# VectorE turns k into token rows by 36 block transpositions; TensorE turns only v

## What is computed

```python
q, k, v, f, u, bg, cg, ga, gb = _split_cols(h @ w_in, IN_SIZES)   # k and v: 1024 columns, 16 heads x 64
o = lax.map(block, (qb, cb, pb))            # prompt attention over 256 tokens, with forget biases
k_past = cache_k[l][page_table].reshape(Bd, n_pages * PAGE_SIZE, N_HEADS, HEAD_DIM)
o = _sample_attention(q, k, v, cum_all[:, P:], cum_all, k_past, v_past)
kp_l.append(k); vp_l.append(v)              # prompt rows of k and v are outputs
ks_l.append(k); vs_l.append(v)              # and so are the sample rows
```

## Time and profile before

| | us |
|---|---|
| median of 3 runs | 1799.98 |
| lowest and highest | 1797.37 and 1800.78 |
| the profiled execution | 1800.58 |
| its span, first to last instruction | 1799.0 |
| TensorE busy | 1781.4 (99%) |
| VectorE busy | 904.7 (50%) |
| ScalarE busy | 702.3 (39%) |

### The profile page before, as it was taken

One profiled execution on the slowest core, in us unless ns is written; L12 is line 12 of the kernel. 1 busy time (PEld: TensorE's weight loads), 2 busy tenths in 40 slices (PEclk: granted clock), 3 DMA queues, 4 the chain that ended last, 5 costly groups with the idle time before them and its releaser, 6 DMA issues.

```text
span 1799.0 us, 31906 instructions
## 1 busy us (share of the span) xinstructions
PE 1781.4 (99%) x13658; PEld 1678.2 (93%) x13658; DVE 904.7 (50%) x1134; ACT 702.3 (39%) x823; POOL 26.1 (1%) x76
## 2 busy tenths in 40 slices
PE   8999999999999999999999999999999999999999
PEld 6888888897699999998979999999999999999999
DVE  4665662235644344454677344444444445565554
ACT  4433233335643333343354333333333334455454
POOL 0000100001000000000000000000000000000000
PEclk9999999999999999999999999999999999999999
DMA  9987677865654444458836554444444444444441
GB/s 361 393 356 319 225 306 308 346 236 208 242 190 166 164 164 164 164 198 339 327 139 259 193 204 164 164 163 163 163 163 163 163 163 165 165 164 165 165 164 74
DMA packets 59367, 382.38 MB, mean 213 GB/s; under 512 B 6989, under 2 KB 7861, under 8 KB 17159
## 3 DMA queue, kind: packets, MB, share of 16 engines
q1 hardware_dynamic: 57764, 378.27, 56.4%
q0 software_dynamic: 1328, 2.58, 0.4%
q10 hardware_dynamic: 178, 0.13, 0.0%
HBM read 376.15 MB, written 4.81 MB: 212 GB/s over the span
## 4 chain that ended last, share of the span: by engine, by line
PE 96%; DVE 2%; ACT 1%; issue 1%; DMA 1%; POOL 0%; DVEq 0%; ACTq 0%; POOLq 0%
PE bank L663 29%; PE bank L665 28%; PE bank L664 28%; PE bank L673 4%; PE bank L907 1%; DMA ada<-in_w_ada 1%; PE bank L1037 1%; PE bank L681 1%; PE bank L1006 0%; PE bank L692 0%; PE bank L1226 0%; PE bank L976 0%; ACT w_hi L1263 0%; PE bank L1149 0%; PE bank L886 0%
## 5 line engine op out<-in xcount | busy, mean ns | idle before, releaser
L663 PE MATMUL bank<-a_lo,w_hi 128*128 128x288 f32 x3632 | 1081.3, 298 | 4.0 <-DVE w_lo L1723 2.6
L664 PE MATMUL bank<-a_hi,w_hi 128*128 128x288 f32 x3632 | 1072.6, 295 | 0.0
L665 PE MATMUL bank<-a_hi,w_lo 128*128 128x288 f32 x3632 | 1069.0, 294 | 0.0
L1723 DVE TENSOR_TENSOR w_lo<-raw,w_hi 128x2048 fp32r<-128x2048 f32 x240 | 550.0, 2292 | 670.3 <-ACT w_hi L1263 669.7
L1263 ACT CAST w_hi<-raw 128x2048 fp32r<-128x2048 f32 x239 | 455.9, 1908 | 838.2 <-PE bank L665 816.9
L663 PEld LDWEIGHTS bank<-a_lo,w_hi 128*128 128x128 f32 x3632 | 681.6, 188 | 23.0 <-issue 22.0
L665 PEld LDWEIGHTS bank<-a_hi,w_lo 128*128 128x128 f32 x3632 | 684.8, 189 | 0.0
L664 PEld LDWEIGHTS bank<-a_hi,w_hi 128*128 128x128 f32 x3632 | 682.7, 188 | 0.0
L1833 DVE TENSOR_TENSOR a_lo<-hid,a_hi 128x1152 fp32r<-128x1152 f32 x44 | 59.4, 1352 | 12.3 <-ACT a_hi L1283 12.3
L673 PE MATMUL bank<-ada,cT 128*32 128x512 f32 (+1 forms) x608 | 63.3, 551 | 1.4 <-DMA ada<-in_w_ada 1.4
L1283 ACT CAST a_hi<-hid 128x1152 fp32r<-128x1152 f32 x44 | 50.7, 1155 | 0.0
(11 more groups left out here) (361 smaller groups left out, 973.1 us busy)
## 6 DMA issues: line engine op xcount, KB each, us to landing
raw<-in_w_ffn_in SPq DMA_DIRECT2D x88, 1024.0 KB, 4.8
raw<-in_w_in SPq DMA_DIRECT2D x75, 1024.0 KB, 8.4
ada<-in_w_ada SPq DMA_DIRECT2D x60, 1024.0 KB, 9.2
raw<-in_w_ffn_out SPq DMA_DIRECT2D x44, 1024.0 KB, 4.8
ada_o<-in_w_ada SPq DMA_DIRECT2D x24, 1024.0 KB, 9.0
raw<-in_w_o SPq DMA_DIRECT2D x16, 1024.0 KB, 5.0
ada<-in_w_ada SPq DMA_DIRECT2D x16, 512.0 KB, 11.0
raw<-in_cache_k SPq DMA_DIRECT2D x16, 512.0 KB, 4.3
```

The source lines that it names most:

```text
L663: pe.matmul(acc, w_hi[buf][:, a, cols], lo[:, kt, :], start=first and a == 0, stop=False)
L664: pe.matmul(acc, w_hi[buf][:, a, cols], hi[:, kt, :], start=False, stop=False)
L665: mm = pe.matmul(acc, w_lo[buf][:, a, cols], hi[:, kt, :], start=False, stop=last and a == tiles - 1)
L1723: tt(w_lo[buf][:, :, :], raw[s][:, :, :], w_hi[buf][:, :, :].bitcast(F32), ALU.subtract).then_inc(raw_turn, 1)
```

## The change

TensorE no longer turns k. The six tiles of k leave ROWS, and with them their 24 transpositions and the six copies out of PSUM (three on ScalarE, three on VectorE); what is left, now V_ROWS, is numbered anew. turn_suf waits for the sums alone. On VectorE turn_keys(b) turns a block of tokens from kT straight into k_rows, in SBUF: for each 32 tokens (t) and each 32 partitions (q) one instruction that transposes eight 32 x 32 blocks. It is called at u = 21, 22 and 23, behind that slot's split_lo where there is one: 16, 16 and 4 instructions. GpSimd's transfers of k_rows wait for k_turned. No product and no output changes.

```diff
@@ the lists @@
-    ROWS = ([("k", half, b) for half in range(2) for b in range(3)]
-            + [("v", 0, 0), ("v", 0, 1), ("v", 1, 0), ("v", 1, 1), ("v", 0, 2), ("v", 1, 2)])
-    ROW_BANK = (4, 5, 4, 5, 6, 7, 6, 7, 2, 3, 7, 2)
+    V_ROWS = [(0, 0), (0, 1), (1, 0), (1, 1), (0, 2), (1, 2)]
+    V_BANK = (6, 7, 2, 3, 7, 2)
+    QUAD = P // 4
@@ TensorE @@
             def turn_suf():
                 pe.wait_ge(suf_done, 1)
                 pe.wait_ge(cum_done, 1)
-                pe.wait_ge(rowT_a, 1)
-                pe.wait_ge(rowT_d, 1)
...
                 if mt == 1:
-                    pe.wait_ge(rowT_a, 3)
-                    pe.wait_ge(rowT_d, 3)
+                    pe.wait_ge(sufT_done, 1)
                     turn_k(0, (0, 1))
...
                     pe.wait_ge(ada_mods, ADA_MAIN + 1)
-                    pe.wait_ge(bank_turn, BT + MT * (G_QKV + 3))
-                    turn_rows(0)
-                    turn_rows(1)
                 if u == 20:
                     turn_suf()
-                if u == 21:
-                    pe.wait_ge(sufT_done, 1)
-                    pe.wait_ge(bank_turn, BT + MT * (G_QKV + 6))
-                    for n in range(2, 6):
-                        turn_rows(n)
@@ ScalarE @@
-                if u == 20:
-                    copy_row(act, nc.scalar.copy, 0)
...
-                if u == 22:
-                    copy_row(act, nc.scalar.copy, 2)
-                    copy_row(act, nc.scalar.copy, 4)
@@ VectorE @@
+            def turn_keys(b):
+
+                for t in range(min(P, NT - b * P) // QUAD):
+                    at_ = slice(b * P + QUAD * t, b * P + QUAD * t + QUAD)
+                    for q in range(4):
+                        rows = slice(QUAD * q, QUAD * q + QUAD)
+                        dst = k_rows[QUAD * t:QUAD * t + QUAD, b, :].rearrange("p (f n) -> p f n", n=P)[:, :, rows]
+                        ins = nc.vector.transpose(dst, kT[rows, :, at_])
+                ins.then_inc(k_turned, 1)
...
                     copy_sums()
-                    copy_row(dve, nc.vector.tensor_copy, 1)
-                if u == 22:
-                    copy_row(dve, nc.vector.tensor_copy, 3)
-                    copy_row(dve, nc.vector.tensor_copy, 5)
+                if u == 21:
+                    dve.wait_ge(bank_turn, BT + MT * (G_QKV + 6))
+                if u in (21, 22, 23):
+                    turn_keys(u - 21)
             copy_KT(0, 1)
             copy_KT(0, 3)
@@ GpSimd @@
-            pool.wait_ge(rowT_a, 3)
-            pool.wait_ge(rowT_d, 3)
+            pool.wait_ge(k_turned, 3)
             pool.dma_start(k_prompt[0, 0].rearrange("(b p) h d -> p b (h d)", p=P), k_rows[:, 0:2, :]).then_inc(s_kout, 16)
```

More of the change, by code:

```diff
@@ L374, in layer @@
         y_made = sem("y_made")
+        k_turned = sem("k_turned")
         rowT_ps, rowT_a, rowT_d, suf_ps, suf_done, sufT_ps, sufT_done = (sem(n) for n in (
@@ L418, in row_tile @@
         def row_tile(n):
[L420 to L424, removed]
+            half, b = V_ROWS[n]
+            return v_rows[half][:, b, :] if b < 2 else v_new[:, 512 * half:512 * half + 512]
         def copy_row(eng, copy, n):
@@ L429, in copy_row @@
             eng.wait_ge(rowT_ps, n + 1)
-            copy(dst, bank[ROW_BANK[n]][0:dst.shape[0], :]).then_inc((rowT_a, rowT_d)[n % 2], 1)
+            copy(dst, bank[V_BANK[n]][0:dst.shape[0], :]).then_inc((rowT_a, rowT_d)[n % 2], 1)
         def y_tile(n):
@@ L881, in turn_rows @@
             def turn_rows(n):
-                name, half, b = ROWS[n]
+                half, b = V_ROWS[n]
                 rows = min(P, NT - b * P)
                 for j in range(4):
-                    mm = pe.transpose(bank[ROW_BANK[n]][0:rows, j * P:j * P + P],
-                                      (kT if name == "k" else vT)[:, 4 * half + j, b * P:b * P + rows], ident[:, :])
+                    mm = pe.transpose(bank[V_BANK[n]][0:rows, j * P:j * P + P],
+                                      vT[:, 4 * half + j, b * P:b * P + rows], ident[:, :])
                 mm.then_inc(rowT_ps, 1)
@@ L920, in first_rows @@
                     pe.wait_ge(bank_turn, BT + MT * (G_QKV + 4))
-                    turn_rows(6)
-                    turn_rows(7)
+                    turn_rows(0)
+                    turn_rows(1)
             for u in range(QKV):
@@ L1056, in _ @@
             pe.wait_ge(sufT_done, 1)
-            pe.wait_ge(rowT_a, 4)
+            pe.wait_ge(rowT_a, 1)
             sample_scores(0)
             pe.wait_ge(bank_turn, BT + MT * (G_MIX + 1))
[L1060 to L1065, removed]
+            turn_rows(2)
+            turn_rows(3)
+            pe.wait_ge(rowT_d, 1)
+            turn_rows(4)
+            pe.wait_ge(rowT_a, 2)
+            turn_rows(5)
             turn_k(1, (0, 1))
             scores(1)
-            pe.wait_ge(rowT_a, 6)
-            pe.wait_ge(rowT_d, 6)
+            pe.wait_ge(rowT_a, 3)
+            pe.wait_ge(rowT_d, 3)
             turn_p(0, 0)
@@ L1444, in _ @@
                     evict(u, 1)
-                    copy_row(act, nc.scalar.copy, 6)
+                    copy_row(act, nc.scalar.copy, 0)
                     evict(u, 2)
@@ L1507, in _ @@
             exp_head(0, 0)
-            copy_row(act, nc.scalar.copy, 8)
-            copy_row(act, nc.scalar.copy, 10)
+            copy_row(act, nc.scalar.copy, 2)
+            copy_row(act, nc.scalar.copy, 4)
             exp_head(0, 1)
             exp_sample(0)
-            act.wait_ge(rowT_ps, len(ROWS))
+            act.wait_ge(rowT_ps, len(V_ROWS))
             new_keys(1)
@@ L2085, in copy_KT @@
                 if s == 1:
-                    dve.wait_ge(rowT_ps, len(ROWS))
+                    dve.wait_ge(rowT_ps, len(V_ROWS))
                 if s > 1:
@@ L2127, in _ @@
                     copy_sums()
-                    copy_row(dve, nc.vector.tensor_copy, 1)
-                if u == 22:
-                    copy_row(dve, nc.vector.tensor_copy, 3)
-                    copy_row(dve, nc.vector.tensor_copy, 5)
+                if u == 21:
+                    dve.wait_ge(bank_turn, BT + MT * (G_QKV + 6))
+                if u in (21, 22, 23):
+                    turn_keys(u - 21)
             copy_KT(0, 1)
             copy_KT(0, 3)
-            copy_row(dve, nc.vector.tensor_copy, 7)
+            copy_row(dve, nc.vector.tensor_copy, 1)
             def max_head(s, j):
@@ L2195, in _ @@
             max_sample(0)
-            copy_row(dve, nc.vector.tensor_copy, 9)
+            copy_row(dve, nc.vector.tensor_copy, 3)
             norm_head(0, 0)
-            copy_row(dve, nc.vector.tensor_copy, 11)
+            copy_row(dve, nc.vector.tensor_copy, 5)
             copy_KT(1, 1)
@@ L2607, in _ @@
             samples_q(1)
-            pool.wait_ge(rowT_a, 6)
-            pool.wait_ge(rowT_d, 6)
+            pool.wait_ge(rowT_a, 3)
+            pool.wait_ge(rowT_d, 3)
             for half in range(2):
```

## The result

| | median of the runs, us | ratio to before | 95% interval |
|---|---|---|---|
| before (17 runs) | 1799.84 | | |
| the change (17 runs) | 1803.02 | 1.0020 | 1.0014 to 1.0027 |

The change makes the kernel slower by 3.2 us (2.5 to 4.9 by the interval); the forecast was 2.5 us, 1802.5 in place of 1803.02. The profiled execution took 1802.74 us against 1800.58, with a span of 1801.2 us against 1799.0.

The account below looks back on a forecast made before the run. TensorE, busy 99% of the span, was taken as the bound; 3.50 us of new wait less 2.45 saved plus 1.47 for the clock gave +2.5 us, 1802.5 us on the median's scale, range 1798.3 to 1807.0.

Parts of the forecast that it names:

- What goes from TensorE: 24 transpositions of k leave TensorE's queue up to slot 22, saving 0.79 + 1.66 = 2.45 us.
- The length of a transposition: On VectorE, each of 36 transpositions takes about 0.44 us from start to start, with no overlap.
- The break-even: The time per VectorE transposition at which TensorE's new wait equals its saving: 0.41 us.
- The wait: TensorE waits 3.50 us for bank 5 ahead of turn_k's fourth group, until VectorE's late KTs copy releases it.
- The clock: Behind TensorE's new wait the clock falls to 0.50, slowing 14 matmuls, for about 1.5 us.
- The sum: New TensorE wait less saving, +1.05 us, plus 1.47 us for the clock: +2.5 us.
- Usual overlap: VectorE transpositions overlap and take 0.34 us each; TensorE waits 1.05 us, net gain 1.4 us; chance 0.15.
- full cover: VectorE transpositions take at most 0.287 us and fit the gaps, so the whole 2.45 us are won; chance 0.05.
- slow transpositions: VectorE transpositions take 0.70 us each, costing +12 us; chance 0.30 with everything from 0.47 us up.
- The rival that the clock stays up: TensorE has the same wait for bank 5 but no clock fall: +1.05 us; chance 0.12.
- Other moved steps: Later k_rows transfers, with 7 us of room before ScalarE's L1496, and later page loads cost nothing.
- rival 3: The last twenty VectorE transpositions fit between 407.59 and 413.34, so the whole 2.45 us are won; chance 0.05.

Follow-up runs that it names:

- e1: The changed kernel with no transpositions of k on VectorE, GpSimd writing zeros for the k rows: 1797.50 us, 0.9989 of before.
- e3: The changed kernel with the twenty late transpositions spread over four places on VectorE's queue: 1796.54 us, 0.9987 of before.
- e2: The changed kernel with each transposition reading the group of 32 partitions it writes, k rows misplaced: 1798.83 us, 0.9995 of before.
- e4b: The changed kernel with seven matmuls of ones run on TensorE in its wait for bank 5: 1801.23 us, 1.0006 of before.
- e5: The changed kernel with turn_keys' two loops swapped, so reads stay in one partition group while the written group changes: 1803.64 us, 1.0022 of before.
- e6: The changed kernel with eight of the second block's sixteen transpositions moved ahead of w_lo of slot 23: 1801.00 us, 1.0010 of before.
- e7: The changed kernel with only the last four transpositions moved behind KTs' first copy: 1799.62 us, 1.0000 of before.

## Why the prediction was right

- **What goes from TensorE** was put at 2.45 us; e1 and e3 measure 2.54. The step that the first eight transpositions are not won whole held: L874 still waits 0.43 us, now for the sums, and starts 0.80 us earlier on the measure above (0.79 forecast).
- **The length of a transposition** was the step on which all hung, taken at 0.44 us from the row of a like instruction (422 ns) and the pair without overlap. It is 436 ns long and 0.45 us from start to start (398.44 to 405.65 for sixteen). The nearest row by number of elements, and the pair for the overlap, were the right two to read. But the 422 ns were those of an instruction without a hold, and a transposition without one takes 394 ns (e2); that the hold also lengthens it stood in no term. The break-even stood at 0.41 us: with the usual overlap the change would have won, as e2, 0.35 us on average, did in its trace (−1.20 us).
- **The wait** was put at 3.50 us and is 3.61; its place, its releaser and its cause are those of the sum. The two numbers don't count the same, though. The row counts from the end of the third group. The sum counted from when the fourth could start, 0.43 us behind the third (413.27): by that it is 3.77 us, 0.27 more than forecast. The 36 starts at 0.45 us in place of 0.44 add 0.36 us, the copy and its release take 0.15 us less than the 0.84 counted, and the rest is that TensorE got there a little sooner. W_lo of slot 23 came some 0.7 us late (405.65, against 404.87 in e1) where 0.45 was forecast, and cost nothing, as said.
- **The clock** was put at 1.5 us from a fall elsewhere and measured 1.32 us by e4b. That the size came so near is in part luck: e5's fall behind the same wait cost 1.34 us more, e6's next to nothing.
- **The sum** of 2.5 us met 2.61 us in the trace, with two misses that partly cancel: 1.05 us for wait less saving measures 1.29, and 1.47 us for the clock 1.32. The median says 3.2 us, with 2.5 still at the edge of its interval. The profiled executions differ by 2.16 us; the rest is that the one of before lies 0.74 us above its median of 17 runs (the prediction had counted 0.60 from three) and the one of the change 0.28 below. The granted clocks of the timed runs point at the reason. In the 33 runs of before beside e4b to e7, those at a mean clock of 0.997 took 1800.7 to 1801.3 us and those at 1.00 took 1796.9 to 1797.5. All seventeen of the change stand at 0.996 or 0.997. So the median of before is taken over executions with more falls and with fewer, and that of the change over executions that all have them. Whether the change makes the falls elsewhere more frequent stays open.
- **Rivals.** Usual overlap and full cover fell with 0.45 us; slow transpositions too: 436 ns for 256 numbers is little more than the 422 ns of L1972, and not the 0.70 us of half the rate. The rival that the clock stays up fell in the traced execution. In the timed runs it isn't seen either, as far as the mean clocks of 0.996 and 0.997 tell: an execution with only the falls of e1's (at the start and near 941 us) has 0.998.
- **Other moved steps** had no cost, e3 with its transfers later still included. The chances had 0.63 on a change within 0.2%; the ratio of 1.0020 lies on that bound.

## What to carry to other kernels

Work taken from the bound engine is not saved if it is queued, on the engine that receives it, ahead of a step for which the bound engine waits. Count the receiver's idle time gap by gap and not as a sum: VectorE was half idle in the whole and had 5.75 us of room (rival 3 of the prediction) in the one gap into which 9 us were put; the same twenty transpositions spread over four gaps won what was meant. Price small instructions at their full length where each starts in another group of 32 partitions than the one in front. And ask what the clock does behind a new wait of TensorE: here it fell behind waits of 1.94 us and more, at a price between nothing and 2.7 us.

## What the runs showed of the hardware

Transpositions of 32 x 256 float32 numbers on VectorE take 436 ns and start 0.45 us apart where each changes its group of 32 partitions on either side (the change, e5). In a row that stays in its groups they take 394 ns and start 0.33 us apart (e2).

The clock behind a wait of TensorE is not a fixed price. It fell at the end of waits of 2.25, 3.60 and 3.61 us and a microsecond behind the end of one of 1.94 us, and not with those of 0.58 and 1.1 us, each seen in one execution. And the wait of 2.64 us of the earlier trace rows, which all these kernels have, behaves in both ways. In the kernel before, and then in e3_spread, the first microseconds behind it:

```profile
944.00:946.00 2.00, 2.00 (x11) 2.00 (x12) 2.00 (x4) 0.22 (x1) 0.00 (x0) 0.62 0.54 164
```

```profile
942.00:944.00 2.00, 2.00 (x17) 2.00 (x17) 2.00 (x6) 1.29 (x4) 0.00 (x0) 1.00 0.91 324
944.00:946.00 2.00, 2.00 (x17) 2.00 (x17) 2.00 (x2) 0.43 (x2) 0.00 (x0) 1.00 0.38 160
```

With the clock up, the rest of the span behind the stretch is 1376.3 us in e3_spread and e6_two_waits; where it fell, 1377.5 to 1377.9 us in all others. Another fall stands at the start: from 10 to 20 us the granted clock is 0.70 in before and 0.69 in e4b_filled_seven and 0.83 to 0.84 in the others, and in those two w_lo of slot 21 starts latest (388.61 and 388.66; the others 387.80 to 388.33). These 1.2 to 1.6 us and few tenths come and go with the execution. They are as large as the effects studied here, and a reason to compare stretches of the trace before whole times.
